# Mixed layer: the convolution's taps computed by VectorE in place of GpSimd, with fewer search rounds beside them

## The reference

```python
h = gate_c * a_in                       # short convolution, 256 channels
y = causal_depthwise_conv3(h, conv_w)   # three taps per channel
ya = gate_b * y
yb = pool_mixer(pv, pool_w, pool_scale) # trailing means over 2, 4, 8, 16 tokens
score = sum_h iw[h] * relu(iq[h] @ ik.T) * idx_scale   # index scores, 8 heads
sel = top_k(score, 128)                 # per query, among its causal keys
yc = attention over the selected keys only, 4 heads
yd = attention over all causal keys (MoBA), 4 heads
mix = concat(ya, yb, yc, yd) @ w_out
```

## Time and profile before

| | us |
|---|---|
| median of 3 runs | 1698.3 |
| lowest, highest | 1696.96, 1699.55 |
| the profiled execution, its time | 1696.41 |
| the profiled execution, its span | 1694.3 |
| mean granted TensorE clock | 0.998 |

### The profile page before, as it was taken

One profiled execution on the slowest core, in us unless ns is written; L12 is line 12 of the kernel. 1 busy time (PEld: TensorE's weight loads), 2 busy tenths in 40 slices (PEclk: granted clock), 3 DMA queues, 4 the chain that ended last, 5 costly groups with the idle time before them and its releaser, 6 DMA issues.

```text
span 1694.3 us, 24289 instructions
## 1 busy us (share of the span) xinstructions
PE 1654.3 (98%) x9349; PEld 1343.5 (79%) x9349; DVE 785.9 (46%) x2038; ACT 767.5 (45%) x1565; POOL 613.0 (36%) x298
## 2 busy tenths in 40 slices
PE   8999999999999999999999998999999999999998
PEld 7777779777888787778777788777788888888877
DVE  3777636566344434435777635888141111001052
ACT  4566634566243535524566634336753222222252
POOL 4323223332242323224322224693144444444423
PEclk9999999999999999999999999999999999999999
DMA  6322144323442312144222145432153333332322
GB/s 170 69 45 73 50 154 137 77 67 64 147 145 75 88 51 78 59 162 112 61 50 75 51 149 148 122 88 75 38 174 100 99 92 95 100 100 88 124 63 87
DMA packets 216047, 161.17 MB, mean 95 GB/s; under 512 B 53756, under 2 KB 197148, under 8 KB 215933
## 3 DMA queue, kind: packets, MB, share of 16 engines
q1 hardware_dynamic: 205904, 130.21, 27.5%
q10 hardware_dynamic: 9804, 29.38, 5.4%
q0 software_dynamic: 224, 0.03, 0.1%
HBM read 148.32 MB, written 11.14 MB: 94 GB/s over the span
## 4 chain that ended last, share of the span: by engine, by line
PE 81%; DVE 9%; ACT 6%; issue 2%; POOL 1%; DMA 0%; ACTq 0%; SPq 0%; DVEq 0%; POOLq 0%
PE banks L481 22%; PE banks L483 22%; PE banks L482 22%; PE banks L739 5%; PE banks L700 4%; PE banks L754 4%; PE banks L905 1%; PE banks L723 1%; ACT G L1613 1%; ACT AB L1484 1%; ACT w_hi L1354 1%; DVE misc L2622 1%; DVE AB L2228 1%; POOL w_lo L2817 1%; DVE QKl L2052 1%
## 5 line engine op out<-in xcount | busy, mean ns | idle before, releaser
L2817 POOL TENSOR_TENSOR w_lo<-w_raw,w_hi 128x1024 fp32r<-128x1024 f32 (+2 forms) x253 | 572.3, 2271 | 1050.6 <-ACT w_hi L1354 1039.4
L481 PE MATMUL banks<-XTh,w_hi 128*128 128x512 f32 (+5 forms) x1216 | 450.7, 371 | 7.2 <-DVE XTl L2287 2.0
L483 PE MATMUL banks<-XTh,w_lo 128*128 128x512 f32 (+5 forms) x1216 | 444.7, 366 | 0.0
L482 PE MATMUL banks<-XTl,w_hi 128*128 128x512 f32 (+5 forms) x1216 | 444.7, 366 | 0.0
L1354 ACT ACTIVATE w_hi<-w_raw 128x1024 fp32r<-128x1024 f32 (+4 forms) x254 | 250.3, 995 | 160.3 <-PE banks L483 107.7
L481 PEld LDWEIGHTS banks<-XTh,w_hi 128*128 128x128 f32 (+2 forms) x1216 | 228.2, 188 | 53.2 <-issue 11.2
L483 PEld LDWEIGHTS banks<-XTh,w_lo 128*128 128x128 f32 (+2 forms) x1216 | 228.2, 188 | 38.1
L482 PEld LDWEIGHTS banks<-XTl,w_hi 128*128 128x128 f32 (+2 forms) x1216 | 228.4, 188 | 36.1 <-issue 0.2
L481 PE MATMUL banks<-w_hi,OTh 128*128 128x512 f32 (+1 forms) x448 | 173.1, 386 | 1.9 <-DVE QKl L2052 1.8
L483 PE MATMUL banks<-w_hi,OTl 128*128 128x512 f32 (+1 forms) x448 | 167.9, 375 | 0.0
L482 PE MATMUL banks<-w_lo,OTh 128*128 128x512 f32 (+1 forms) x448 | 167.8, 375 | 0.0
(11 more groups left out here) (212 smaller groups left out, 2340.8 us busy)
## 6 DMA issues: line engine op xcount, KB each, us to landing
w_raw<-in_w_gate_up_dram SPq DMA_DIRECT2D x44, 512.0 KB, 3.8
w_raw<-in_fox_w_in_dram SPq DMA_DIRECT2D x30, 512.0 KB, 4.1
w_raw<-in_mla_w_in_dram SPq DMA_DIRECT2D x26, 512.0 KB, 4.9
w_raw<-in_w_in_dram SPq DMA_DIRECT2D x24, 512.0 KB, 3.9
w_raw<-in_w_down_dram SPq DMA_DIRECT2D x22, 512.0 KB, 3.5
w_raw<-in_swa_w_in_dram SPq DMA_DIRECT2D x20, 512.0 KB, 4.2
w_raw<-in_mla_w_out_dram SPq DMA_DIRECT2D x16, 512.0 KB, 3.7
x_spill<-AB ACTq DMA_DIRECT2D x16, 512.0 KB, 2.6
```

The source lines that it names most:

```text
L481: nc.tensor.matmul(o, ah, bh, start=first, stop=False, skip_group_check=True)
L482: nc.tensor.matmul(o, ah, bl, start=False, stop=False, skip_group_check=True)
L483: return nc.tensor.matmul(o, al, bh, start=False, stop=last, skip_group_check=True)
L2817: pool.tensor_tensor(view(w_lo, u, RING), view(w_raw, u, RAW), view(w_hi, u, RING).bitcast(F32), ALU.subtract).then_inc(lo_done, 1)
```

## The change

VectorE takes over the taps: one `tensor_scalar` for tap 0 and one `scalar_tensor_tensor` (multiply by the tap's weight and add) for each of taps 1 and 2, right behind the product with gate C, each waiting for the one before. `conv_taps` on GpSimd, the semaphore `conv_s` and the two waits on it go. The calls of `top` around the third index block of each convolution take fewer rounds: 3 and 3 become none and 2 in the first, 0 and 4 become none and 2 in the second. The other calls keep their numbers, and `top(48)` takes what is left. Lines of the changed kernel lie some lines off those of the kernel before.

```diff
--- before.py
+++ after.py
@@ -315,7 +315,7 @@
         kr_done = sem("kr_done")
         rope_done = sem("rope_done")
         ident_round, sel_done = sem("ident_round"), sem("sel_done")
-        conv_s, conv_lo = sem("conv_s"), sem("conv_lo")
+        conv_lo = sem("conv_lo")
         pool_s1 = sem("pool_s1")
         fx, fx_m, fz_done = sem("fx"), sem("fx_m"), sem("fz_done")
         idx_s, idx_r, idx_f = sem("idx_s"), sem("idx_r"), sem("idx_f")
@@ -1962,8 +1962,6 @@
                 if n:
                     idx_block(n)
                 advance()
-                if n == 3:
-                    act.wait_ge(conv_s, 4)
                 if n % 3 == 0:
                     stored(nc.scalar.activation(CONV_A, group()[:, :], ACT.Copy))
                 else:
@@ -2644,11 +2642,14 @@
                 o = group()
                 groups_stored(dve, c.g - 1)
                 stored(nc.vector.tensor_tensor(CONV_H[:, 2:514], o[:, :], CONV_A, ALU.mult))
-                top(0 if cc else 3)
+                groups_stored(dve, c.g)
+                link(nc.vector.tensor_scalar(CONV_Y, CONV_H[:, 0:512], conv_w[:, cc, 0:1], None, ALU.mult))
+                for tap in (1, 2):
+                    link(nc.vector.scalar_tensor_tensor(CONV_Y, CONV_H[:, tap:tap + 512], conv_w[:, cc, tap:tap + 1], CONV_Y,
+                                                        ALU.mult, ALU.add))
                 idx_block(3 * cc + 2)
-                top(4 if cc else 3)
+                top(2)
                 o = group()
-                dve.wait_ge(conv_s, 4 * cc + 4)
                 if cc:
                     dve.wait_ge(conv_lo, cc)
                 stored(nc.vector.tensor_tensor(otmp[:, :], o[:, :], CONV_Y, ALU.mult))
@@ -2793,17 +2794,6 @@
 
             conv0 = next(u for u, x in enumerate(units) if x[0] == "conv")
 
-            def conv_taps(cc):
-
-                pool.wait_ge(cst, N_CST)
-                groups_stored(pool, mark["conv", cc])
-                pool.tensor_scalar(CONV_Y, CONV_H[:, 0:512], conv_w[:, cc, 0:1], None, ALU.mult)
-                for tap in (1, 2):
-                    pool.tensor_scalar(CONV_A, CONV_H[:, tap:tap + 512], conv_w[:, cc, tap:tap + 1], None, ALU.mult).then_inc(conv_s, 1)
-                    pool.wait_ge(conv_s, 4 * cc + 2 * tap - 1)
-                    pool.tensor_tensor(CONV_Y, CONV_Y, CONV_A, ALU.add).then_inc(conv_s, 1)
-                    pool.wait_ge(conv_s, 4 * cc + 2 * tap)
-
             def conv_low(cc):
 
                 pool.wait_ge(g_hi, mark["conv_hi", cc])
@@ -2822,9 +2812,7 @@
                 elif u < 3 + len(CONSTANTS):
                     dst, src = CONSTANTS[u - 3]
                     pool.dma_start(dst, src).then_inc(cst, 16)
-                if u in (conv0 + 4, conv0 + 7):
-                    conv_taps((u - conv0 - 4) // 3)
-                elif u in (conv0 + 6, conv0 + 9):
+                if u in (conv0 + 6, conv0 + 9):
                     conv_low((u - conv0 - 6) // 3)
                 if u == pool0 + 3:
                     window_sums(0)
```

## The result

The changed kernel takes 1710.14 us (median of 4 runs, 1707.65 to 1711.49), the kernel before in the same sessions 1697.63 us (4 runs, 1696.66 to 1699.55). The ratio is 1.0068 with a 95% interval of 1.0053 to 1.0083: **slower by 11.5 us, 9 to 14**. The forecast was 1707.0 us in a range of 1703.0 to 1710.5, with 0.91 on slower: the time lies 3.1 us above the forecast and just inside the range. A second set of 5 rounds gave 1709.03 against 1699.25, ratio 1.0060 (1.0046 to 1.0074), which is 10.2 us (2.0 us above the forecast).

What follows compares the result with a forecast made beforehand. The prediction took TensorE, busy 1654.3 of 1694.3 us, as the bound. The last call's delay gave +7.6 us with g counted, the clock made it 8.7; 1696.4 + 8.7 + 1.9 for the median gave 1707.0 us, range 1703.0 to 1710.5.

Steps and rivals of the forecast that it cites:

- The search rounds: Last call of top: six more rounds of 1.517 us, +9.1 us on VectorE; the call ends 7.6 us later.
- g: How much earlier VectorE's second product, and so L1161, comes: 1.2 us, with bounds 0 and 1.98.
- Who waits for it: Third pair's third group of scores (L700): TensorE stands 8.5 us behind the last call; +7.6 us in total.
- Rival D: Third group does not wait for the last call: 1696.3 us; chance 0.11 together with its middle case.
- middle case: Last call starts some 3 us sooner than forecast: 5.7 us, 1704.0; chance within rival D's 0.11.
- E: The change does not do what its words say: eight rounds move, 12.1 us, 3.0 more; no separate chance given.
- The clock: Behind the L700 wait: 3.3 us at half rate, 1.65 us lost, less 0.46 of wait; 8.7 in place of 7.6.
- Rival A: Behind the L700 wait the clock costs nothing, ScalarE's path alone decides: 7.6 us, 1705.9; chance 0.14.
- Rival B: Clock stays low from 1179.37 to 1185.88, 6.5 us of work takes 13: 13.5 us, 1711.8; chance 0.05.
- The taps: On VectorE before the second product: 2.1 us per convolution; with rounds taken out, 2.1 us earlier, 0.9 given to GpSimd's splits.
- rival C: A GpSimd split holds the second convolution's taps by 1.9 us: g becomes -0.7, total 10.6, 1708.9; chance 0.12.
- The direction: Whole kernel: slower with chance 0.91, same 0.06, faster 0.03.

Runs made afterwards that it cites:

- repeat: The changed kernel itself, timed and profiled again in 5 rounds against the kernel before; 1709.03 us, ratio 1.0060.
- e1: Kernel before with only the smaller numbers of search rounds (2 + 2 before the second product), taps left on GpSimd; 1707.49 us, ratio 1.0045.
- e6: Changed kernel with one GpSimd weight split held back until the sixth index block's sums are done; 1706.02 us, ratio 1.0042.
- e4: Changed kernel with all six rounds put into three calls ahead of the last (3, 3, 13 become 4, 5, 16); 1703.18 us, ratio 1.0020.
- filler: Changed kernel with 35 matmuls of unused result put before the third group of scores to keep TensorE busy; 1709.5 us, ratio 1.0056.
- e2: Changed kernel with the search rounds where the kernel before has them, so only the taps move to VectorE; 1703.76 us, ratio 1.0026.
- e9: Changed kernel with the rounds where the kernel before has them and the second convolution's GpSimd split held back; 1701.80 us, ratio 1.0014.
- e5: Kernel before with two rounds of the first convolution moved into two later calls, taps on GpSimd; 1698.35 us, ratio 0.9998.
- e10: Changed kernel with the six rounds spread over earlier calls (4, 5, 16) and the GpSimd split held back; 1702.26 us, ratio 1.0014.

## Why the prediction was right, and where it was off

**The search rounds: right.** The order's six rounds, their price of 1.517 us and their landing in the last call all stand in the timeline of the changed kernel. That the call's start is tied to TensorE and not to VectorE's own work is shown by the wait, which is 8.50 or 8.51 us in four profiles (the change, its repeat, e1, e6) whose TensorE was from 1.6 us ahead (e1) to 1.1 behind (the repeat) at L1161, counted from the sixth block; in all four VectorE waited 1.15 us for the rounded tile ahead of the call. The forecast's "the last call ends 7.6 us later" came out as 9.3: the mask stands 94.63 us behind the start of the sixth block in place of 85.32. Counted from L1161 it is 8.73 later, against 9.1 - 0.3 = 8.8; the rest is g, which was a loss.

**Who waits for it: right.** 8.5 us was forecast, 8.51 measured, and 61.98 us became 70.59. Nothing gave it back later. Rival D is out, its middle case too: the stand is there in full, and without the taps as well (e1). With the six rounds spread over earlier calls (e4), another wait takes its place. E is out by the twelve rounds.

**The clock: right in the net.** Forecast were 3.3 us at half rate, 1.65 us lost, less 0.46 of wait. The trace has some 4.7 us at half. From the third group to the transposes at L739 that costs 2.2 us (6.08 us in place of 3.86). Given back are 0.61 ahead of the next six transposes, where 0.46 was counted, and 0.30 in them: they took 1.11 us in the kernel before, with small gaps, as in the filler's timeline above, and 0.82 in the changed one. That makes 1.3, and on the ruler, from the third group to the end, it is +1.30; the filler gives back 1.11 of it, and the forecast's net was 1.19. So more work was lost than forecast and more given back, and that the net fits is in part luck. It is also not a constant: in the repeat, the change, e6 and e1, all with the same stand, the clock was at half for 4.0, 4.7, 5.3 and 6.1 us behind it, and this last stretch was 0.88, 1.30, 1.57 and 1.87 us longer than before. Rival A (nothing) is out, by the filler's ruler and not by its median. Rival B (half rate throughout, 6.5 us) is out: in 1198 to 1200 the clock is at full, and that is where L739's transposes begin (1199.05). The Trainium skill (TensorE: Matmul & The Clock Gate, Part 4) says that transposes do not count as activity in the way that products do; here the clock came back on the products ahead of them, so no run tested that rule.

**The taps and g: the term that was mis-sized.** "I give 0.9 of the 2.1 to that. The product comes g = 1.2 us earlier." Measured is g = -0.58, and -1.09 in the repeat. The 10.5 us on the ruler less the 8.7 forecast are 1.8 us, and they are all here (1.2 + 0.58). The taps themselves cost what was counted. What was too small is the 0.9 for VectorE standing beside GpSimd's splits, and it falls in both convolutions. From the product with gate C to the product with gate B:

| | counted without splits | measured | difference |
|---|---|---|---|
| first convolution | 1.8 earlier | 0.87 earlier (9.45 in place of 10.32) | 0.9 |
| second convolution | 0.3 earlier | 1.43 later (10.95 in place of 9.52) | 1.75 |

The second row is shown by experiment: with that split held back (e6) the stretch is 8.94 us and g is a gain of 1.16. That this is the forecast's 1.2 is luck: the forecast had already charged 0.9 for splits, and in e6 the first convolution's split still costs about that (4.22 us for the three multiply-adds, as in the change). The first row is read from the traces alone; no run here held that split back by itself. Where no GpSimd instruction runs beside them (e2), the three take 2.06 us:

```profile
1078.97 2.06 DVE L2620 SCALAR_TENSOR_TENSOR misc<-AB,iw_t,misc 128x384 f32<-128x384 f32 x3
```

So each meeting takes 2.0 to 2.2 us. What it costs against the kernel before is less, 1.06 and 1.54 us (another 0.2 in the second row is a longer gap ahead of the first tap), because there the old taps on GpSimd already slowed the same multiply-adds (3.16 and 3.79 us in place of 2.06 and 3.32). The forecast counted neither.

The price of 1.9 us stood in rival C, from the earlier trace rows, for one more meeting on top of the 0.9. Its sum, 10.6, is within 0.1 us of the ruler. In the first profile of the changed kernel the split did not meet the taps, C's place, but the index multiply-adds. In the repeat of the very same kernel it did meet the taps, as C had it (L2648 took 3.55 us in place of 1.54, and the index multiply-adds 3.32), and likewise in e2. The stretch from gate C to gate B was 10.94 us, the same as in the first profile. Which instruction is met changes from one execution to the next; the price of the meeting did not.

The view of one line's instructions (durations in ns: least, median, greatest) shows where the 2.0 us fall, in the changed kernel from 1099 to 1106 us and in e2 from 1097 to 1103:

```profile
L2620 DVE SCALAR_TENSOR_TENSOR misc<-AB,iw_t,misc x4: 751/752/2767, 1100.6 to 1105.2; 128x512 f32<-128x512 f32 x4
```

```profile
L2648 DVE SCALAR_TENSOR_TENSOR AB<-AB,conv_w x2: 752/1761/2770, 1098.5 to 1099.3; 128x512 f32<-128x512 f32 x2
```

One instruction is held for 2.0 us and its neighbours not at all. The split ran until 1102.83 (1099.98 and 2.85), so it had 2.2 us left when the first multiply-add began at 1100.61. The Trainium skill (SBUF — State Buffer, SBUF: two separate sides) describes such a lock, exclusive and held for a whole instruction, for a VectorE instruction with two SBUF inputs beside a GpSimd one that reads SBUF; the trace agrees, with 2.77 us against 0.75.

**The direction: right.** Against the medians the change costs 11.5 or 10.2 us, on the ruler 10.5, and 8.7 was forecast. The halves do not add up: e1 and e2 cost +8.9 and +6.1 on the ruler, the change 10.5. e2 keeps two more rounds ahead of the second product than the change does (and four more in the first convolution), stands for 4.0 us there and loses some 2.7 us of work at half rate behind it. With the rounds moved, the taps on VectorE cost 10.5 - 8.9 = 1.6 us more than leaving them on GpSimd (2.2 up to L1161; e1 then lost 0.6 more to the clock).

## What to carry to other kernels

Deferred work lands in the call that takes all that is left: count what arrives there, at that call's price, and see what hangs behind its end, whatever the engine's busy share says. When work moves from GpSimd to VectorE, list which of GpSimd's remaining instructions will now run beside VectorE's, in every stage that the change touches, and price each meeting by what is left of the GpSimd instruction when VectorE's begins (2.0 to 2.2 us for a split met at its start), less what the same instructions already paid before the change. For spans that differ ahead of the change, compare from a point just before it.

## What the hardware showed unexpectedly

**The clock falls after some waits of 1.5 to 2 us and not after others, and spans differ by that ahead of the change.** All profiled executions have a wait of 1.57 us at about 1047. Behind it the granted clock fell in four of twelve. Where it did not, TensorE came earlier to L1133, waited about 3 us instead of 1.8 there, and in seven of those eight the clock fell then. The stretches, of the kernel before and of the changed kernel (the clock is the third number from the end):

```profile
1046.00:1052.00 6.00, 5.63 (x31) 5.63 (x32) 1.90 (x4) 2.51 (x4) 4.72 (x2) 0.72 0.78 230
1056.00:1066.00 10.00, 9.05 (x57) 7.30 (x58) 4.84 (x9) 5.72 (x15) 4.72 (x3) 1.00 1.10 276
```

```profile
1046.00:1052.00 6.00, 4.43 (x35) 4.00 (x34) 2.87 (x5) 4.12 (x7) 3.34 (x2) 1.00 0.49 154
1058.00:1068.00 10.00, 9.31 (x39) 7.55 (x39) 3.02 (x7) 3.44 (x9) 4.49 (x2) 0.66 1.04 267
```

From the first to the second index block this makes 6.58 us against 9.14. An earlier place adds to it: at 320, behind waits of 0.77 and 0.87 us, the clock fell for some 3 us in seven of the twelve (the changed kernel among them, the kernel before and the repeat not). The sixth block starts at 1091.5 to 1096.0 us over the twelve, nearly as wide as the spread of the kernel before's own runs (1696.5 to 1701.6). The same holds behind the change: after waits of 2.10 us (e4), 2.04 (e9), and 1.01 and 0.73 close together (e5) the clock fell for some 3.4 us, after 2.13 (e10) it did not. What decides it stays open. A forecast that removes or adds a wait of 1.5 to 2 us must carry about 1.7 us of clock (an estimate: half of 3.4) on either side.

**GpSimd is held as well, and single-input instructions of VectorE too.** The split beside the index sums began while VectorE was still in its second fused tap instruction and took 2.85 us, where the next of its size took 2.41 (from 1111.05). So the meeting cost VectorE 2.0 us and GpSimd 0.4. In the repeat a split that began at 1074.13 met the tensor_scalar of L2617 (from 1074.09), which has one tensor input: it took 2.64 us in place of 0.42.
